# A mixture-of-experts layer: the row lists of turns 20 on are built once through memory, and gathers leave out rows of padding

## What is computed

```python
_, top_e = lax.top_k(sel, TOP_K)                 # 8 of 64 experts for each token
wts = scores of these, scaled to a sum of 2.5
for each block of rows of one expert e:
    xb = x_pad[rows]                             # gathered tokens
    hb = jax.nn.silu(xb @ w_gate[e]) * (xb @ w_up[e])
    y = y.at[rows].add((hb @ w_down[e]) * wb[:, None])
```

## Time and profile before

| | us |
|---|---|
| median of 3 runs (2834.76 to 2840.95) | 2837.86 |
| the profiled execution's own time | 2834.48 |
| its span, first to last instruction | 2832.7 |
| turns of layer 0, from 781 us | 778 |
| turns of layer 1, from 1976 us | 768 |

### The profile page before, as it was taken

The page is one execution under the profiler, slowest core; times in us unless marked ns, Lnnn a source line. Parts: engine busy times, 40 slices in busy tenths (PEclk is TensorE's granted clock), DMA queues, the critical chain, the costliest instruction groups (busy, mean ns, idle before and its releaser), DMA issues. The chain is left out here.

```text
span 2832.7 us, 40293 instructions
## 1 busy us (share of the span) xinstructions
PE 2671.8 (94%) x13974; PEld 1212.0 (43%) x13975; DVE 1864.6 (66%) x3373; ACT 1429.0 (50%) x3340; POOL 501.7 (18%) x404
## 2 busy tenths in 40 slices
PE   7998999899899999999999698997999999999994
PEld 3444666445333443434433264443333334333332
DVE  4996555576667666666665555766666667677655
ACT  1113555332166666666665241332656666666653
POOL 0000000111022222222222121100222222222212
PEclk9999999999999999999999799998999999999997
DMA  9777300201499999999999622016999999999996
GB/s 363 261 269 208 141 16 9 81 30 45 181 363 346 331 320 349 362 353 345 377 336 325 221 103 88 30 45 261 328 311 357 320 376 350 345 377 295 334 338 208
DMA packets 147093, 714.98 MB, mean 252 GB/s; under 512 B 16702, under 2 KB 22078, under 8 KB 94665
## 3 DMA queue, kind: packets, MB, share of 16 engines
q1 hardware_dynamic: 104252, 556.14, 50.1%
q0 software_dynamic: 42336, 154.16, 21.2%
q10 hardware_dynamic: 304, 2.11, 0.2%
HBM read 597.50 MB, written 114.84 MB: 251 GB/s over the span
## 5 line engine op out<-in xcount | busy, mean ns | idle before, releaser
L1692 ACT ACTIVATE xT<-xt_blocks 32x256 f32<-32x256 f32 x2208 | 913.9, 414 | 42.6 <-DVE xt_blocks L1559 14.8
L1771 PE MATMUL exG<-ring,xT 128*32 128x512 f32 (+2 forms) x2352 | 699.4, 597 | 2.9 <-DMA ring<-in_exp_w_up_dram 2.4
L1771 PEld LDWEIGHTS exG<-ring,xT 128*32 128x32 f32 (+2 forms) x2352 | 231.9, 141 | 308.0 <-issue 303.9
L1805 PE MATMUL exD<-ring,ex_hT 128*32 128x512 f32 (+2 forms) x1176 | 355.8, 606 | 2.4 <-DVE w_o L1597 1.2
L1564 DVE TENSOR_SCALAR ex_e<-ex_e 128x256 f32<-128x256 f32 x142 | 43.4, 306 | 426.9 <-ACT ex_e L1704 426.6
L1565 DVE RECIPROCAL ex_e<-ex_e 128x256 f32<-128x256 f32 x142 | 248.9, 1753 | 4.9
L1704 ACT ACTIVATE ex_e<-exG 128x256 f32<-128x256 f32 x142 | 54.4, 383 | 315.0 <-PE exG L1771 315.0
L1771 PE MATMUL exG<-oT,xT 128*32 128x512 f32 (+2 forms) x592 | 197.8, 600 | 1.0 <-DVE xT L1553 1.0
L1771 PE MATMUL exG<-w_fnet,xT 128*32 128x512 f32 (+2 forms) x608 | 176.7, 600 | 2.4 <-DMA ring<-in_exp_w_up_dram 2.4
L1523 DVE TENSOR_TENSOR mod<-place,slots 128x1024 bf16<-128x1024 f32 (+3 forms) x196 | 174.1, 912 | 4.5 <-PEq L234 3.6
L1805 PEld LDWEIGHTS exD<-ring,ex_hT 128*32 128x32 f32 (+2 forms) x1176 | 116.4, 142 | 128.7 <-issue 127.8
(11 more groups left out here) (424 smaller groups left out, 4319.2 us busy)
## 6 DMA issues: line engine op xcount, KB each, us to landing
ring<-in_exp_w_gate_dram SPq DMA_DIRECT2D x64, 1024.0 KB, 10.8
ring<-in_exp_w_up_dram SPq DMA_DIRECT2D x64, 1024.0 KB, 14.9
ring<-in_exp_w_down_dram SPq DMA_DIRECT2D x64, 1024.0 KB, 9.2
ada_w<-in_w_ada_dram SPq DMA_DIRECT2D x48, 512.0 KB, 5.6
oT<-in_exp_w_gate_dram SPq DMA_DIRECT2D x17, 1024.0 KB, 9.9
oT<-in_exp_w_up_dram SPq DMA_DIRECT2D x17, 1024.0 KB, 13.9
oT<-in_exp_w_down_dram SPq DMA_DIRECT2D x17, 1024.0 KB, 9.3
fT<-in_exp_w_gate_dram SPq DMA_DIRECT2D x17, 1024.0 KB, 10.4
```

Source lines behind the costliest of these rows:

```text
L1692: last = act.activation(xT[m * UNIT:(m + 1) * UNIT, par, :, a * UNIT:(a + 1) * UNIT], parts[a * UNIT:(a + 1) * UNIT, m], ACT.Copy)
L1771: last = pe.matmul(psG[par][p:p + m], xT[:, par, k, p:p + m], ring[s % RING][:, 0:2, k * FF:(k + 1) * FF], start=k == 0, stop=k == KT - 1)
L1805: last = pe.matmul(psD[p:p + m, c], hT[:, k * P + p:k * P + p + m], ring[s % RING][:, 2, k * D + c * 512:k * D + (c + 1) * 512], start=k = ...
```

## The change

**The lists.** In VectorE's iteration 1, `slot_keys` makes for each token and expert a key: where in the lists the pair's row stands. In iteration 2, `slot_rows` takes the eight keys of each token (`max`) and turns them into addresses. In iterations 3 to 10, `slot_weights` picks the eight weights of each token. In GpSimd's iterations 4 to 13, 64 indirect DMAs (6 or 7 in each, behind that iteration's add) each write 128 entries of two numbers (token, weight) to their addresses in `list_dram`. Behind the add of iteration 14 GpSimd waits until all have landed and loads the lists of all turns back with one DMA. VectorE waits for it in iteration 15, ahead of `hidden(15)`, and makes the gather rows and the target rows of all turns.

**Turns 20 on.** `onehot`, `index`, `indices` and `targets` are no longer made for turns 20 to 70; gathers, adds and weighings take their columns of the lists. The overflow blocks still make their own.

**Beside that.** The overflow table moves from iteration 9 to 17. Routing gains one copy of 128x512 from PSUM (the weights), ahead of the last four operations. Each gather has a bound, the last token's row; rows past it are not fetched, and what the buffer held stays. Two small DMAs on SP at each expert stage's start bring constants, and two in the kernel's first stage fill the lists with empty entries. GpSimd makes two more iotas at the stage's start.

```diff
@@ routing, the end of VectorE's series
                         dve.sem_inc(idx_done, 1)
+                        dve.tensor_copy(mod[:, 3 * D:3 * D + NT * E].rearrange("p (t e) -> p t e", e=E), psM[:, :, E:])
                         link(tt(rest, psM[:, :, E:], moving[:, :, :, 3], ALU.subtract))
@@ first stage, SP
+                        for l in range(DEPTH):
+                            sp.dma_start(list_dram[l][:, SENDS:].rearrange("p t c -> p (t c)"), A["list_empty"][l]).then_inc(emptied, 16)
@@ experts, SP
+                        sp.dma_start(base, A["list_base"][layer:layer + 1].to_broadcast([P, E])).then_inc(base_in, 16)
+                        sp.dma_start(half, A["list_half"][layer]).then_inc(half_in, 16)
@@ experts, GpSimd
+                        def send(first_entry, last_entry):
+                            for c in range(first_entry, last_entry):
+                                t, j = divmod(c, TOP_K)
+                                pool.wait_ge(entries_done, t + 1)
...
+                                pool.indirect_dma_start(out=list_dram[layer].rearrange("p t c -> (p t) c"),
+                                                        out_offset=bass.IndirectOffsetOnAxis(ap=slot_at[:, c:c + 1], axis=0),
+                                                        in_=entries[:, t, j], in_offset=None).then_inc(listed, 16)
                         def gather(b, par, lag):
-                            pool.wait_ge(idx_done, b + 1)
+                            listed_row = isinstance(b, int) and LIST <= b < T
+                            if listed_row:
+                                pool.wait_ge(list_ready, 2)
+                            else:
+                                pool.wait_ge(idx_done, nth(b) + 1)
...
+                                                    bounds_check=SEQ - 1, oob_is_err=False
                                                     ).then_inc(gathered[par], 16)
...
                             add(b - 1, (b - 1) % 2)
+                            i = b - SEND_FROM
+                            if 0 <= i < SEND_IN:
+                                send(SENDS * i // SEND_IN, SENDS * (i + 1) // SEND_IN)
+                            if i == SEND_IN:
+                                pool.wait_ge(listed, 16 * SENDS)
+                                pool.dma_start(spare[:, 512:512 + 2 * T], list_dram[layer][:, SENDS:].rearrange("p t c -> p (t c)")
+                                               ).then_inc(list_in, 16)
@@ experts, VectorE
+                        def slot_keys():
...
+                            list_link(dve.tensor_tensor(part, place[:], wide(caps[:]), ALU.is_lt))
+                            list_link(dve.scalar_tensor_tensor(out=part, in0=place[:], scalar=0.0, in1=part, op0=ALU.is_ge, op1=ALU.mult))
+                            list_link(dve.tensor_tensor(key, place[:], wide(base), ALU.add))
+                            list_link(dve.tensor_tensor(key, key, part, ALU.mult))
+                        def slot_weights(t):
+                            for j in range(TOP_K):
+                                last = dve.scalar_tensor_tensor(out=part[:, j], in0=key[:, t], scalar=slot8[:, t, j:j + 1], in1=wts[:, t],
+                                                                op0=ALU.is_equal, op1=ALU.mult)
+                            list_link(last)
+                            list_link(dve.tensor_reduce(entries[:, t, :, 1], part, AX, ALU.add))
+                            dve.sem_inc(entries_done, 1)
+                        def slot_lists():
+                            dve.wait_ge(list_in, 16)
+                            dve.wait_ge(half_in, 16)
+                            dve.tensor_copy(row_at, lists[:, :, 0]).then_inc(list_ready, 1)
...
                         for b in range(1, T):
                             par = b % 2
-                            if b == 9:
+                            if b == 17:
                                 overflow()
-                            if b + AHEAD < T:
+                            if b + AHEAD < LIST:
                                 onehot(b + AHEAD, par)
...
+                            if b == 1:
+                                slot_keys()
+                            elif b == 2:
+                                slot_rows()
+                            elif b < NT + 3:
+                                slot_weights(b - 3)
+                            elif b == SEND_FROM + SEND_IN + 1:
+                                slot_lists()
                             hidden(b, par, 2)
...
-                            targets(b - 1, 1 - par, max(0, b - 2) * 16)
+                            if b - 1 < LIST:
+                                targets(b - 1, 1 - par, max(0, b - 2) * 16)
```

More of the change, by code:

```diff
@@ L60 @@
 TABLE = 256
+SENDS = NT * TOP_K
 KSLOTS = NT + 2 + CT
@@ L141, in pieces, with list_constants @@
     return [(s, r, p, m) for s, r, _, at, n in turn for p in range(at, at + n, m)]
+def list_constants():
+    f = np.float32
+    p = np.arange(P)
+    base, upper, empty = [], [], []
+    for layer in range(DEPTH):
+        turns, _, _ = schedule(layer)
+        at, half = np.zeros(EXPERTS, f), np.zeros((P, len(turns)), f)
+        for b, turn in enumerate(turns):
+            for i, (_, r, done, row, n) in enumerate(turn):
+                if done == 0:
+                    at[r] = (b + SENDS) * P + row
+                half[row:row + n, b] = i
+        none = np.zeros((P, len(turns), 2), f)
+        none[:, :, 0] = DUMMY + p[:, None]
+        base.append(at)
+        upper.append(half)
+        empty.append(none.reshape(P, -1))
+    return {"list_base": np.stack(base), "list_half": np.stack(upper), "list_empty": np.stack(empty)}
 def constants():
@@ L199, in constants @@
         "caps": np.asarray(UNITS, f) * UNIT,
+        **list_constants(),
     }
@@ L209, in trunk @@
     row_dram = dram("row_scratch", [2, 2 * D])
+    list_dram = [dram(f"list_scratch{l}", [P, SENDS + len(schedule(l)[0]), 2]) for l in range(DEPTH)]
     table_dram = dram("table_scratch", [BLOCKS, 4], I32)
@@ L1415, in experts, with nth @@
                 HAND, AHEAD, SPLIT, Q = 2, 4, 5, P // UNIT
+                LIST, SEND_FROM, SEND_IN = 20, 4, 10
+                spare = mod[:, 3 * D:5 * D]
+                wts = spare[:, 0:512].rearrange("p (t e) -> p t e", e=E)
+                key = spare[:, 512:1024].rearrange("p (t e) -> p t e", e=E)
+                part = spare[:, 1024:1536].rearrange("p (t e) -> p t e", e=E)
+                slot8 = spare[:, 1536:1600].rearrange("p (t j) -> p t j", j=TOP_K)
+                slot_at = spare[:, 1600:1664].bitcast(U32)
+                line, rank8 = spare[:, 1664:1728], spare[:, 1728:1792]
+                entries = spare[:, 1792:1920].rearrange("p (t j c) -> p t j c", j=TOP_K, c=2)
+                base, nowhere, half = spare[:, 1920:1984], spare[:, 1984:2048], mod[:, D:D + T]
+                lists = spare[:, 512:512 + 2 * T].rearrange("p (t c) -> p t c", c=2)
+                row_at, sum_at = (mod[:, 3 * D + 768 + i * P:3 * D + 768 + i * P + T].bitcast(U32) for i in range(2))
+                base_in, half_in, list_own, entries_done, listed, list_in, list_ready, numbered = (sem(n) for n in (
+                    "list_base_in", "list_half_in", "list_own", "entries_done", "listed", "list_in", "list_ready", "numbered"))
+                def nth(b):
+                    return b if isinstance(b, int) and b < LIST else b - T + LIST
                 def rows_read(eng, b):
@@ L1494, in add @@
                             pool.wait_ge(y_done, b + 1)
-                            pool.wait_ge(out_idx, b + 1)
+                            listed_row = isinstance(b, int) and LIST <= b < T
+                            if not listed_row:
+                                pool.wait_ge(out_idx, nth(b) + 1)
                             at_least(pool, added, b * 16)
@@ L1596, in weigh @@
                             at_least(dve, added, before)
-                            dve.scalar_tensor_tensor(out=yo[:, par], in0=psD[:].rearrange("p a b -> p (a b)"), scalar=w_all[:, ds(b, 1)], in1=gate2,
+                            by = lists[:, b, 1:2] if LIST <= b < T else w_all[:, ds(b, 1)]
+                            dve.scalar_tensor_tensor(out=yo[:, par], in0=psD[:].rearrange("p a b -> p (a b)"), scalar=by, in1=gate2,
                                                      op0=ALU.mult, op1=ALU.mult).then_inc(y_done, 1)
@@ new lines, in slot_rows @@
+                        def slot_rows():
+                            for t in range(NT):
+                                last = dve.max(slot8[:, t], key[:, t])
+                            list_link(last)
+                            keys8 = slot8.rearrange("p t j -> p (t j)")
+                            dve.wait_ge(numbered, 2)
+                            list_link(dve.tensor_tensor(keys8, keys8, nowhere, ALU.max))
+                            list_link(dve.tensor_copy(slot_at, keys8))
```

(11 more changed lines are left out.)

33 lines of the change are left out of this document (24 added, 9 removed).

## The result

| | median us | runs | lowest to highest |
|---|---|---|---|
| before | 2838.24 | 4 | 2834.76 to 2840.95 |
| after | 2866.32 | 4 | 2863.49 to 2870.77 |

What follows compares the result with a forecast made beforehand. TensorE was taken as the bound, the DMA engines right behind. A layer: -14.8 - 5.7 + 0.7 + 14.3 = -5.5; two layers -11, +3 for DMA, forecast -8, so 2830 us on the median; range 2795 to 2878.

Steps and rivals of the forecast that it cites:

- The sends, which decide the case: GpSimd's 64 sends a layer, turns 4 to 13, at 1.25 us each; late lists cost 14.3 us a layer.
- rival (b): GpSimd falls behind: gain gone at 1.31 us a send; 2912 us at 1.89, half-way 2871; chance 0.31.
- (c): DMA engines become the bound, shorter turns partly spent waiting for weights: +6 to the forecast, 2836 us; chance 0.13.
- If turns 5 to 14 stretch beyond 11.3: Sign of a wrong forecast in the send turns: beyond 11.3 us, GpSimd or the queue is the bound there.
- Index products: TensorE's index product dropped in turns 20 to 70: 0.29 us a turn, 14.8 us a layer gained.
- Overflow table: Table moved from iteration 9 to 17: long turn at 9 goes, none at 17; 5.7 us a layer gained.
- Routing copy, stage start, slot work of VectorE: Copy at routing's end +0.7 us a layer; stage-start loads 0, at most 1 together; VectorE's slot work hidden.
- Gathers without padding: At least a tenth of a gather's rows goes, but TensorE never waits for gathers in the steady part: nothing booked.
- Load of the lists: Issued 12.7 us into iteration 15, landing about 22; hidden may start by 9.8; stall 12, with surroundings 14.3 a layer.
- DMA engines: In heavy stretches the DMA engines can't follow the shorter turn of 10.83 us and take some gain back: +3 us.
- The adds themselves just hold: During the sends GpSimd's turn is 12.1 us against 11.12; adds fall back from 1.3 to 11, limit 10.5.
- second form of rival (b): `slot_weights` on VectorE locks GpSimd as the one-hot does: 1.0 us a turn, 7 a layer, 2844 us; chance 0.13.

Runs made afterwards that it cites:

- u_sends: Changed kernel with the lists written and loaded but read by no turn, index products kept: 2890.0 us, again 2898.6 on another chip.
- u_no_sends: u_sends with all 64 sends a layer left out: 2836.8 us, 0.9995 of the kernel before.
- a_no_bound: Changed kernel without the bound on the gathers, so rows of padding are read too: 2837.0 us, 0.9997 of the kernel before.
- a_late_lists: Changed kernel with the lists taken over in iteration 18 instead of 15 and used from turn 23: 2826.0 us, on another chip 2867.7.
- a_thin: Changed kernel with sends spread over 20 turns, lists taken over in iteration 28, used from turn 33: 2821.3 us, 0.9943 of the kernel before.
- a_thin_table: a_thin with the overflow table built in iteration 31 instead of 17, its loads later in SyncE's queue: 2812.0 us, again 2812.8 on another chip.
- u_thin: u_sends with the 64 sends a layer spread over 30 turns, lists taken over at iteration 37: 2838.8 us, 1.0008 of the kernel before.
- u_direct: u_sends with each indirect send replaced by a direct transfer of the same 128 entries: 2836.0 us, again 2836.6 and 2838.2 on other chips.

## Why the prediction was wrong

**The step that failed** is the one named "The sends, which decide the case". It counted a send as GpSimd's time alone: an issue, and a place in the queue. That price was right, 0.96 + 0.30 = 1.27 us from start to start against 1.25 forecast, also in the changed kernel. What it had no term for is what a dense row of them does to TensorE. The runs put it at 53 us for 128 sends (u_sends less u_no_sends, chip A). It falls neither under rival (b), whose price hung on a send of 1.31 us or more, nor under (c): the DMA share in the long turn was 0.30. "If turns 5 to 14 stretch beyond 11.3 (then GpSimd or the queue is the bound there)" named the sign rightly and read it wrongly. The direction was wrong with it. That the range held the time is luck: its upper part was there for dearer sends, and the sends weren't dearer.

**How 53 us became 29.** Against a_no_bound the changed kernel loses 22.3 + 32.6 = 55 us in intervals 6 to 14 and gets back 9.5 + 18.1 = 28 in 15 to 17, since a chain that is already late waits less for the lists. The medians differ by 2866.3 - 2837.0 = 29. So the wait for the lists and the long turns cover each other in part, and a_late_lists on chip C, with later lists but the same sends, gained 5 us over the changed kernel there (2867.7 against 2872.8), where 22 were expected.

**The other steps**, one by one:
- Index products: forecast 0.29 us a turn and 14.8 a layer; intervals 18 to 71, which hold 49 of the 51, give 597.8 - 584.4 = 13.4 and 13.0, so 0.27 us a turn. Right, slightly over.
- Overflow table: the long turn at 9 went (a_no_bound has 11.1 there) and none came at 17 in a version without index products behind it. u_no_sends shows the reason was the right one: with the products the stall is back, 16.65 us for the turn. a_thin (17.39 in interval 17) and a_thin_table_again (11.25) show it again. In layer 1, though, not all of it was to be had: in interval 14 a longer wait for weights takes back 0.5 us of the 6.3 (u_thin), 3 (u_no_sends) or nearly all (a_thin_table, where intervals 6 to 14 take 108.4 us, against 108.8 before). That is the prediction's rival (c), the full DMA engines, in one turn; against it stood the +3 in the sum.
- Routing copy, stage start, slot work of VectorE: u_no_sends is at 2836.8. Its table at 17 costs what the one at 9 did (5.4 us in layer 0), and layer 1 has the 3 us of interval 14 on top, so nothing that can be measured is left for these three to cost. Right.
- Gathers without padding: q0, the queue of GpSimd's transfers, moved 154.16 MB before and 145.09 after; a_no_bound, with 154.44, took no measurably longer than before. Nothing speaks against the booking of nothing, but no two kernels on one chip differ in the bound alone.
- Load of the lists: forecast 12.7 us into iteration 15, on a_no_bound 959.63 - 943.99 = 15.6. The stall was mis-sized: 14.3 a layer forecast; a_no_bound has 50.2 - 33.4 = 16.8 and 54.5 - 33.2 = 21.3. The lists came when forecast (21.7 us into the iteration), so it was the slack that was wrong. TensorE asked for `hidden(15)` 9.5 us into the iteration, not 13.4, because the iteration was itself late: GpSimd's gathers had fallen behind (24.5 us of waiting for `xt_blocks`). And TensorE came back at a lower clock. In spans, a_no_bound is 4.6 us longer than the kernel before (2837.3 against 2832.7), where -8 was forecast. Of the 12.6 between them the stall has 9.5 and the late intervals 6 to 14 have 4.8 (103.5 and 104.1 against 105.5 - 5.2 and 108.8 - 6.3); intervals 1 to 5 give 0.7 back (the last 1 us isn't assigned). So even on a chip without long turns the outcome would have been no change that can be measured.
- DMA engines: +3 booked; the late turns saved 3.2 us less in all than 51 products a layer at 0.29 us, about 2 less for the 49 in them. The size fits, but no run shows that the DMA engines are the reason.
- Send phase of GpSimd: 12.1 us a turn forecast. "The adds themselves just hold" was nearly so: on a_no_bound intervals 12 to 14 are 1.2, 1.1 and 0.9 us longer in layer 0 (12.30, 11.88, 11.94), 0.5, 0 and 0.9 in layer 1. The second form of rival (b), a lock by `slot_weights`, isn't there: 128 sends took 127.0 us in all, 4 more than 128 times the usual 0.96.

**What stays open.** By which path a dense row of indirect transfers holds TensorE, why direct ones don't (the form, or the shorter row), and what differs between the chips. One rival was not tried: the recording itself. Each execution here, also one that only gave a time, has a span and a granted clock on record, so it was profiled. And the chips on which the sends hurt are those on which records go missing, also in kernels that aren't slowed (a_thin_table_again on E has 1,776 of the 2,048 records of its sends, a_thin_table on D 2,040). Whether writing the records slows TensorE, or the same thing slows both, or neither, no run here tells; so it isn't shown that the 53 us are there in an execution without a profile. The Trainium skill (DMA: Bandwidth & Descriptors, SWDGE vs HWDGE vs iDMA) says that GpSimd builds the descriptors of its direct and indirect transfers alike and puts them into rings that lie in SBUF. By that rule alone u_direct should have hurt as well, and on chip E it did not; whether the rings have a part in it, no run here shows. No kernel had the bound as its only difference on a chip with long turns, so the bound isn't excluded as a part of it.

## What to carry to other kernels

Spread indirect transfers that nobody waits for: on some chips 6 or 7 small ones in a row per 11 us turn cost 53 us for 128, while 3 or 4 per turn brought no long turn, and fewer rows in each don't help. When a transfer's cost is estimated from GpSimd's pace and its landing, ask besides what it does to engines that have nothing to do with it, and run the version on more than one chip before believing a gain. Work that stalls others should be moved behind the last work that waits for it, and a hand-over placed by the time its data lands: two late lists cost 16.8 + 21.3 us on a_no_bound, and using them later costs about 0.27 us a turn.

## What the runs showed of the hardware that I had not expected

- A dense row of indirect transfers from GpSimd slows TensorE on some chips and not on others: the same kernel took 2867.7 and 2826.0 us, at a granted clock of 1.00 in the slowed stretch shown. The kernel before differed by less than 1 us there.
- The number of rows hardly counts: GpSimd took 0.84 us for a send of 16 rows and 0.96 for 128, and both left as 16 packets (46,496 in q0 with either). The slowdown of TensorE went up with the smaller ones, 72 us instead of 53.
- A direct transfer of the same 128 entries is issued every 0.5 to 0.6 us on GpSimd, an indirect one every 1.27.
- Where TensorE is slowed like this, records of completions go missing from the trace (656 of 2,048 were there), and waits read "remote". On the same chips some go missing without any slowing (1,776 to 1,933 of 2,048 there, 2,025 to 2,040 on B and D), so the number tells the two kinds of chip apart in every trace here.
- With the long turn at 9 gone, a wait for weights five turns later grew from 2.35 to 3.98 us (layer 1, DMA share 1.02 and 1.01 around it).
